# When a modulation chain rests, how the first FFN ends, and who casts the first weight tiles

## The chip, the cores and the metric

The kernel runs on one core of a Trainium2 chip, in one launch. The metric is the device time of a run in microseconds; less is better. The core has TensorE (PE in the profile; PEld is its weight load), VectorE (DVE), ScalarE (ACT), GpSimd (POOL) and SyncE (SP), each of which takes its instructions in order and waits for others by semaphores. SyncE issues nearly all DMAs, from one queue.

## The reference

Two blocks over 256 tokens of width 1024, batch 1, all in float32. The first mixes an mLSTM with a sparse attention and adds a gated projection. The second has two layers; each computes

- `mod = silu(c) @ mod_w[i] + mod_b[i]`, six vectors of 1024, numbered (i, m): 0 and 1 shift and scale the mixer's input, 3 and 4 the FFN's, 2 and 5 gate the two branches
- `hin = x * (1 + mod1) + mod0`, then a mixer: layer 0 MLA (compress `hin` to `c_q` and `c_kv` by one product, rms-normalise them, expand to queries, keys and values, rotary part by a product of its own, causal softmax attention of 8 heads, output product), layer 1 MoBA, which for 256 tokens is causal attention with position penalty
- `x = layer_norm(alpha * x + mod2 * y)`, then `hin = x * (1 + mod4) + mod3`, a convolutional gated FFN of inner width 2816 (`ffn_a`, `ffn_b`, a 3-tap convolution, gelu, product, `ffn_o`), and `x = layer_norm(alpha * x + mod5 * y)`

## The kernel before, in words

Every large product is made of three matmuls: a float32 operand is split into a high half (a cast to fp32r) and a low half (the rest), and high*high + high*low + low*high are accumulated. Weights arrive as tiles of 128x1024 (512 KB), numbered in the order of use by `weight_units` (line 61). For each tile SyncE loads it into a slot of the ring (`load`), ScalarE casts it (`hi`, line 1861), VectorE subtracts (`lo`, line 1330), and TensorE uses it (lines 1099 to 1101). Four to six `parts` hold tiles that are split; a slot of the ring is free again after its `lo`.

The order of all work is one list of steps that `order` (line 102) builds before anything runs; each engine walks the list and issues what is its own, so a step's place in the list is its place in the queue of every engine that it touches. The class `Stream` (`W`) keeps it: `next` is called for the tile wanted now; it first prepares tiles ahead while a part is free (`prepare`: load and `hi`), and emits `lo` until at most `lag` prepared tiles are without one (`low`). `done` gives a part back and calls `step`, which advances the tasks that run beside: each has a rate, and for every whole one that its account reaches, one step of the task is emitted. `W.still` stops the emission while the account goes on.

One such task is `modulation` (the chain): for the vectors (0, 0), (0, 1), (0, 3), (0, 4), (1, 0), (1, 1), (1, 3), (1, 4) it emits eight `mod_v` steps (VectorE, lines 1389 and 1391: the weight tile times a scalar, added to an accumulator), then two empty steps (one in layer 1), `mod_one` with `mod_sum`, and `mod_pe` with `mod_fin`. Its rate is `mod[0][1]`, from `MOD_PACE`. It is 0 from the gate product of the first block on and is set to 0.65 right after `modulated(0, 0)` (line 780). The vectors (i, 2) and (i, 5) are made otherwise: `Between` loads eight `mod_w` tiles and TensorE multiplies them (`mod_k`, line 1182) in the waits around a normalisation, `tiles` saying how many where. One of its loads goes into `R2`, which is free after `mod_one` of (0, 4). `until` forces out what is left of a vector that is needed.

The MLA begins with `modulated(0, 0)` (transposes of x into `XT` with scale and shift), `mla_c` (tiles 76 to 79, row by row, evacuated by `ev_cq`, lines 1794 and 1799), `mla_kr` (tiles 80 and 81, evacuated by `rope`, lines 1806 and 1808), the transposes of `cq` (line 1112) with `xt_s` (ScalarE high, line 1879; VectorE low, line 1349), and `mla_uv` (tiles 82 and 83, evacuated by `ev_v`).

The FFN of layer 0 uses tiles 98 to 163. `LAST` says up to which round the `ffn_o` tiles (`fo` steps) follow a round later; what is left is done in `last`, where the residual `resid` follows each output: `res_m` (line 1754), `res_a` (1763), `res_s` (statistics, 1768), the variance's end (1775, 1778, GpSimd 2207, 1784) and the normalisation `ln_fin` (VectorE 1788, ScalarE 2086). Four outputs (t, cb): row block t of 128 tokens, column half cb. Before, only tiles 162 and 163 were in `last`.

At the start x is rms-normalised (`rms1`: ScalarE 1866 and 1870, VectorE 1336 and 1340, GpSimd 2159), transposed into `XT` (`xt_s`), and tiles 0 and 1 are split by hand: 0 on VectorE alone (1324 and 1330), 1 on GpSimd alone (2147 and 2153). The first product `blk2` takes them in turns: four k of tile 0, four of tile 1, and again. `busy` (line 1120) are matmuls of zeros.

Of the kernel before, what the change touches and what calls it, by code (L numbers as in the profile page):

```python
# [28 lines left out]
LAG = 1  # L29

LAST = [10, 8]
# [70 lines left out]
def order():  # L102
# [34 lines left out]
    class Stream:  # L137
# [25 lines left out]

        def next(self, name, u):
            while len(self.ready) < min(self.at + len(part.uses) - len(lost), len(units)) and part.free:
                self.prepare()
                while len(self.ready) - self.lows > self.lag:
                    self.low()
            while self.lows <= self.at:
                self.low()  # L170
            while self.soon:
                self.soon.pop(0)()
            assert units[self.at][0:2] == (name, u), (units[self.at], name, u)
            self.at += 1
            return self.at - 1, self.ready[self.at - 1][1]
# [80 lines left out]
    def transposed(tag, nk, kind, ks=None, apart=False, filled=()):  # L256
# [15 lines left out]
        for k in ks or range(0, nk, 2):  # L272
            if apart:
                b = banks[k]
                add("tr", tag, k, (1,), b, None)
            else:
                b = bank.get()
                add("tr", tag, k, (0, 1), b, prior("bank", b))
            if kind is None:
                add("xt_hl", tag, k, b)  # L280
                bank.put(b[0])
            elif kind == "s":
                add("xt_s", tag, k, b)
                bank.put(b[0])
            else:
                s = wk.get()
                add("xt_m", tag, k, b, s, prior("wk", s))
                bank.put(b[0])
                pending.append((k, s))
                if len(pending) > 1:  # L290
                    low_part()
        while pending:
            low_part()
# [14 lines left out]
    add("in_b")  # L308
    add("zero")
# [4 lines left out]
    for on in "VG":  # L314
        W.prepare(on)
        W.low(on)
    transposed("u", 8, "s", apart=True, filled=(lambda: add("busy", 1, 5, bz), lambda: add("busy", 2, 5, bz)))
# [353 lines left out]
    def modulated(i, which, v=None, tiles=()):  # L671
# [7 lines left out]
        transposed(f"m{i}{which}", 8, "m", apart=True, filled=(lambda: v.tiles(tiles[1]), lambda: v.tiles(tiles[2])))  # L679
# [33 lines left out]
    def ffn(i):  # L713
# [14 lines left out]
        def last():  # L728
# [15 lines left out]
            for cb in range(2):  # L744
                for j in js[-2:]:
                    piece(0, cb, j)
            for cb in range(2):
                for j in js:
                    piece(1, cb, j)
            for j in js:  # L750
# [29 lines left out]
    mod[0][1] = MOD_PACE[1]  # L780
# [7 lines left out]
    proj_a("m00", 8, "mla_c", 0, 1, ev_cq)  # L788

# [6 lines left out]
    transposed("cq", 4, "s", ks=(2, 0))  # L796

# [57 lines left out]
    modulated(1, 0, late[0], (3, 3, 2))  # L855
# [39 lines left out]
def build(nc, D, out):  # L895
# [4 lines left out]
    with ctx:  # L900
# [400 lines left out]
        def vector(ve):  # L1301
# [15 lines left out]
            for kind, *a in steps:  # L1317
                if kind == "zero":
                    ve.memset(zero, 0.0).then_inc(*done("V", "zero"))
                elif kind == "hi" and a[5] == "V":  # L1320
                    u, slot, p, before, n, _ = a
                    for e in new("V", ("ld", *slot), before):
                        ve.wait_ge(*e)
                    ve.tensor_copy(parts[p[0]][:, 0:n], raw[slot[0]][:, 0:n]).then_inc(*done("V", "hi", u))
# [7 lines left out]
                elif kind == "rms1":  # L1332
# [5 lines left out]
                    for e in new("V", ("rms1_rs", t)):  # L1338
                        ve.wait_ge(*e)
                    ve.tensor_scalar(Y[:, t, 0:512], X[:, t, 0:512], ss[:, t:t + 1], None, MUL).then_inc(  # L1340
                        *done("V", "rms1", t, 0))
# [513 lines left out]
        def scalar(ac):  # L1855
            for kind, *a in steps:
# [5 lines left out]
                elif kind == "rms1":  # L1862
# [5 lines left out]
                    for e in new("A", ("rms1_rs", t)):  # L1868
                        ac.wait_ge(*e)
                    ac.activation(Y[:, t, 512:1024], X[:, t, 512:1024], ACT.Copy, scale=ss[:, t:t + 1]).then_inc(  # L1870
                        *done("A", "rms1", t, 1))
# [546 lines left out]
```

## Time and profile before

| | us |
|---|---|
| median of 3 runs | 918.39 (917.83 to 918.71) |
| profiled execution | 917.69 |
| its span | 915.9 |
| TensorE busy | 880.1 (96%) |
| VectorE busy | 683.6 (75%) |
| ScalarE busy | 450.2 (49%) |
| GpSimd busy | 70.3 (8%) |
| HBM read | 198.71 MB, 218 GB/s over the span |

Busy time of TensorE counts modelled ends of pipelined matmuls, so a matmul's duration in a row (0.39 us at 512 columns) is longer than its distance to the next one. PEclk is the granted clock, 1.00 being 2.4 GHz and 0.50 being 1.2 GHz. The name before L is the engine, L1330 is line 1330. In a timeline the first number is the start in us from the span's start, the second the duration, and in brackets stands how long the engine was idle before and what ended it.

### The profile page before, as it was taken

The numbers are of one execution on the slowest core, as the hardware profiler recorded it, in microseconds if no ns is written. First come the engines' busy times: TensorE is split into PE (matmuls) and PEld (weight loads), VectorE is DVE, ScalarE is ACT, GpSimd is POOL, SyncE is SP. The second block draws the span as 40 slices with busy tenths as digits, with TensorE's granted clock in tenths as the row PEclk, the third lists the DMA queues.
The fourth block names the chain that finished last, engine by engine and source line by source line (L and its number), as shares of the span: only waits on it lengthen the run. The fifth ranks groups of instructions, "written<-read, shape, count | busy, mean of one in ns | idle before, by whom it ended". The sixth has DMA issues, their size and how long they took to land.

```text
span 915.9 us, 14506 instructions
## 1 busy us (share of the span) xinstructions
PE 880.1 (96%) x5776; PEld 760.4 (83%) x5776; DVE 683.6 (75%) x1084; ACT 450.2 (49%) x712; POOL 70.3 (8%) x64
## 2 busy tenths in 40 slices
PE   8999999999999799989999999989999899999996
PEld 7988887667876697779989999868987799999995
DVE  4697788786996887779867767886787876646666
ACT  5563544444545644455544544354554555444550
POOL 2000001000000110011111010010000120100101
PEclk9999999999999999999999999999999999999999
DMA  8855566544957680399957787648724885665601
GB/s 287 325 170 168 201 202 228 167 143 158 325 207 302 233 318 24 120 345 312 378 184 265 265 323 269 219 152 326 234 93 176 335 309 184 204 201 160 208 3 47
DMA packets 56893, 200.74 MB, mean 219 GB/s; under 512 B 6589, under 2 KB 7925, under 8 KB 56825
## 3 DMA queue, kind: packets, MB, share of 16 engines
q1 hardware_dynamic: 55816, 196.63, 61.4%
q0 software_dynamic: 1008, 3.18, 0.9%
q8 instruction: 46, 0.75, 0.3%
q14 instruction: 23, 0.18, 0.1%
HBM read 198.71 MB, written 1.08 MB: 218 GB/s over the span
## 4 chain that ended last, share of the span: by engine, by line
PE 89%; DVE 6%; issue 2%; ACT 1%; DMA 1%; POOL 1%; SPq 0%; DVEq 0%; ACTq 0%
PE ps L1099 27%; PE ps L1100 26%; PE ps L1101 26%; PE ps L1272 3%; PE ps L1293 1%; PE ps L1112 1%; PE ps L1279 1%; DMA ring<-in_w_iq 1%; PE ps L1233 1%; DVE wk L1366 1%; PE ps L1261 1%; DVE X L1763 1%; PE ps L1191 1%; DVE small L1768 0%; PE ps L1253 0%
## 5 line engine op out<-in xcount | busy, mean ns | idle before, releaser
L1099 PE MATMUL ps<-XT,wsp 128*128 128x256 f32 x768 | 217.2, 283 | 4.3 <-DVE XT L1373 3.0
L1100 PE MATMUL ps<-XT,wsp 128*128 128x256 f32 x768 | 214.6, 279 | 0.0
L1101 PE MATMUL ps<-XT,wsp 128*128 128x256 f32 x768 | 214.2, 279 | 0.0
L1330 DVE TENSOR_TENSOR wsp<-ring,wsp 128x1024 fp32r<-128x1024 f32 x130 | 160.5, 1241 | 17.6 <-ACT wsp L1861 17.6
L1861 ACT CAST wsp<-ring 128x1024 fp32r<-128x1024 f32 (+1 forms) x129 | 134.6, 1046 | 64.6 <-PE ps L1101 52.1
L1099 PEld LDWEIGHTS ps<-XT,wsp 128*128 128x128 f32 x768 | 144.0, 188 | 8.5 <-issue 4.2
L1100 PEld LDWEIGHTS ps<-XT,wsp 128*128 128x128 f32 x768 | 144.0, 188 | 0.9
L1101 PEld LDWEIGHTS ps<-XT,wsp 128*128 128x128 f32 x768 | 143.6, 187 | 0.0
L1099 PE MATMUL ps<-wsp,ra 128*128 128x512 f32 x236 | 95.2, 403 | 6.9 <-issue 5.1
L1101 PE MATMUL ps<-wsp,ra 128*128 128x512 f32 x236 | 94.3, 399 | 0.0
L1330 DVE TENSOR_TENSOR wsp<-arena,wsp 128x1024 fp32r<-128x1024 f32 x74 | 92.6, 1256 | 1.7 <-ACT wsp L1861 1.7
L1100 PE MATMUL ps<-wsp,ra 128*128 128x512 f32 x236 | 93.8, 397 | 0.0
L1861 ACT CAST wsp<-arena 128x1024 fp32r<-128x1024 f32 x74 | 77.1, 1045 | 29.8 <-PE ps L1101 29.6
L1311 DVE SCALAR_TENSOR_TENSOR wk<-ps,cols,wk 128x255 f32<-128x255 f32 (+1 forms) x88 | 36.3, 475 | 69.3 <-ACT wk L2125 69.3
L1099 PE MATMUL ps<-XT,ra 128*128 128x256 f32 x288 | 81.4, 283 | 0.0
L1100 PE MATMUL ps<-XT,ra 128*128 128x256 f32 x288 | 80.8, 281 | 0.0
L1101 PE MATMUL ps<-XT,ra 128*128 128x256 f32 x288 | 80.8, 280 | 0.0
L1099 PE MATMUL ps<-wsp,XT 128*128 128x512 f32 x180 | 73.8, 410 | 1.8 <-issue 1.8
L1100 PE MATMUL ps<-wsp,XT 128*128 128x512 f32 x180 | 71.1, 395 | 0.0
L1101 PE MATMUL ps<-wsp,XT 128*128 128x512 f32 x180 | 71.1, 395 | 0.0
L2225 POOL TENSOR_TENSOR ra<-wk,ra 128x512 fp32r<-128x512 f32 x22 | 37.8, 1718 | 297.5 <-ACT ra L2138 297.5
L1099 PEld LDWEIGHTS ps<-wsp,ra 128*128 128x128 f32 x236 | 44.9, 190 | 18.2 <-issue 6.2
(263 smaller groups left out, 1554.4 us busy)
## 6 DMA issues: line engine op xcount, KB each, us to landing
arena<-in_mod_w SPq DMA_DIRECT2D x48, 512.0 KB, 5.7
ring<-in_mod_w SPq DMA_DIRECT2D x44, 512.0 KB, 4.8
ring<-in_ffn_a SPq DMA_DIRECT2D x30, 512.0 KB, 5.1
arena<-in_ffn_b SPq DMA_DIRECT2D x28, 512.0 KB, 4.8
ring<-in_ffn_o SPq DMA_DIRECT2D x27, 512.0 KB, 4.5
arena<-in_ffn_o SPq DMA_DIRECT2D x17, 512.0 KB, 4.9
ring<-in_ffn_b SPq DMA_DIRECT2D x16, 512.0 KB, 5.1
ring<-in_w_moz SPq DMA_DIRECT2D x14, 512.0 KB, 3.6
```

What stands on the lines that cost most here:

```text
L1099: pe.matmul(o, l[0], r[0], start=start, stop=False)
L1100: pe.matmul(o, l[0], r[1], start=False, stop=False)
L1101: return pe.matmul(o, l[1], r[0], start=False, stop=stop)
L1112: ins = pe.transpose(o, src, ID)
L1191: ins = pe.matmul(ps[b[0]][32 * j:32 * j + 32, 0:256], ones[:, 0:32], acc[q][:, j * 256:(j + 1) * 256], start=True, stop=True, tile_positi ...
L1233: ins = pe.matmul(ps[b[0]][:, e_ * n:(e_ + 1) * n], iqT[r, h // 2, t * 128:(t + 1) * 128], ikT[r, 0:n], start=True, stop=True)
L1261: ins = pe.matmul(ps[b[0]][:, 0:257], pb[es[j][0]][:, c:c + 128], mv[:, j, h, 0:257], start=j == 0, stop=j == t)
L1272: ins = pe.matmul(ps[b[0]][:, 0:n], l, r, start=q == 0, stop=q == len(terms) - 1)
L1311: ve.scalar_tensor_tensor(o[:, sh:256], src[:, q * 256:(q + 1) * 256 - sh], scale(tap, q), o[:, sh:256], MUL, ADD).then_inc(*done("V", top ...
L1330: ve.tensor_tensor(w[:, 1024:1024 + n], raw[slot[0]][:, 0:n], w[:, 0:n].bitcast(f32), SUB).then_inc(*done("V", "lo", u, also=[("raw", *slo ...
L1861: ac.copy(parts[p[0]][:, 0:n], raw[slot[0]][:, 0:n]).then_inc(*done("A", "hi", u))
L2225: po.tensor_tensor(gp[g[0]][:, 512:1024], wk[s[0]], gp[g[0]][:, 0:512].bitcast(f32), SUB).then_inc(*done("G", "ffn_lo", i, u, also=[("wk", ...
```

## The change

Five edits.

1. `mod[0][1] = MOD_PACE[1]` moves from ahead of `mla_c` to behind the transposes of `cq`, and `W.lag` is 2 instead of 1 from behind `mla_c` until there.
2. `LAST[0]` is 9 instead of 10: four tiles (160 to 163) are left for `last` of layer 0. There, in layer 0, row block 1 takes its first two tiles tile by tile and gives their parts back, before the other two are taken output by output.
3. `modulated(1, 0)` gets `W.ahead`, which prepares one tile and emits one `low` if a part is free: once after the second group of `mod_k` tiles and once behind the third pair of transposes. Its tiles are divided (1, 4, 3) instead of (3, 3, 2).
4. At the start tile 0 is cast on ScalarE and tile 1 on GpSimd, both behind the rms normalisation; both low halves are VectorE's, the second behind the `xt_s` of the second pair. GpSimd's cast waits for `rms1` of row block 1. Row block 0 of `rms1` is scaled by VectorE alone.
5. Tiles 3 and 4 are loaded at once, behind the constants, and not after the small inputs.

```diff
-LAST = [10, 8]
+LAST = [9, 8]
...
+        def ahead(self):
+            if part.free and len(self.ready) < len(units):
+                self.prepare()
+                self.low()
...
-    def transposed(tag, nk, kind, ks=None, apart=False, filled=()):
+    def transposed(tag, nk, kind, ks=None, apart=False, filled=(), mid=None):
...
                 bank.put(b[0])
+                if mid and k == 2:
+                    mid()
             else:
...
                 if len(pending) > 1:
                     low_part()
+                if mid and k == 4:
+                    mid()
...
     add("in_b")
+    for _ in range(2):
+        W.fetch()
...
-    for on in "VG":
-        W.prepare(on)
-        W.low(on)
-    transposed("u", 8, "s", apart=True, filled=(lambda: add("busy", 1, 5, bz), lambda: add("busy", 2, 5, bz)))
+    W.prepare()
+    first["part", 1] = ("rms1", 1, 0)
+    W.prepare("G")
+    W.low()
+    transposed("u", 8, "s", apart=True, filled=(lambda: add("busy", 1, 5, bz), lambda: add("busy", 2, 5, bz)), mid=W.low)
...
-    def modulated(i, which, v=None, tiles=()):
+    def modulated(i, which, v=None, tiles=(), ahead=lambda: None):
...
-        transposed(f"m{i}{which}", 8, "m", apart=True, filled=(lambda: v.tiles(tiles[1]), lambda: v.tiles(tiles[2])))
+        transposed(f"m{i}{which}", 8, "m", apart=True, filled=(lambda: (v.tiles(tiles[1]), ahead()),
+                                                               lambda: v.tiles(tiles[2])), mid=ahead)
...
+            free = js[:-2] if i == 0 else []
+            for j in free:
+                for cb in range(2):
+                    piece(1, cb, j)
+                W.done(got[j][1])
             for cb in range(2):
-                for j in js:
+                for j in js[len(free):]:
                     piece(1, cb, j)
-            for j in js:
+            for j in js[len(free):]:
                 W.done(got[j][1])
...
     modulated(0, 0, vs.pop(), (3, 3, 2))
-    mod[0][1] = MOD_PACE[1]
...
     proj_a("m00", 8, "mla_c", 0, 1, ev_cq)
+    W.lag = LAG + 1
...
     transposed("cq", 4, "s", ks=(2, 0))
+    mod[0][1], W.lag = MOD_PACE[1], LAG
...
-    modulated(1, 0, late[0], (3, 3, 2))
+    modulated(1, 0, late[0], (1, 4, 3), W.ahead)
```

## Rows read from the trace of the kernel before

**Rows 1.** The page's part 4, the chain that ended last, by engine.
```profile
PE 89%; DVE 6%; issue 2%; ACT 1%; DMA 1%; POOL 1%; SPq 0%; DVEq 0%; ACTq 0%
```
**Rows 2.** Stretches of one microsecond: length, busy time by engine, granted clock, DMA.
```profile
317.00:318.00 1.00, 0.00 (x0) 0.00 (x0) 1.00 (x2) 0.84 (x1) 0.17 (x1) 1.00 0.66 184
318.00:319.00 1.00, 0.00 (x0) 0.00 (x0) 1.00 (x2) 0.00 (x0) 0.00 (x0) 0.56 0.96 393
...
323.00:324.00 1.00, 1.00 (x4) 0.71 (x4) 0.95 (x2) 0.00 (x0) 0.00 (x0) 0.50 1.03 422
```
**Rows 3.** TensorE's timeline, 312 to 331: start, duration, instruction.
```profile
314.51 1.23 PE L1112 MATMUL ps<-cst,arena 128*128 128x128 f32 x8
320.85 0.77 PE L1099 MATMUL ps<-wsp,ra 128*128 128x512 f32 x1 [5.11 <-issue]
...
324.82 0.45 PE L1099 MATMUL ps<-wsp,ra 128*128 128x512 f32 x1
325.12 0.39 PE L1100 MATMUL ps<-wsp,ra 128*128 128x512 f32 x1
...
328.15 0.39 PE L1101 MATMUL ps<-wsp,ra 128*128 128x512 f32 x1
```
**Rows 4.** VectorE's timeline over the same stretch.
```profile
313.82 0.88 DVE L1799 TENSOR_SCALAR arena<-ps,small 128x256 f32<-128x256 f32 x2 [0.82 <-POOL small L2213]
314.62 1.27 DVE L1391 SCALAR_TENSOR_TENSOR R<-ring,cactr,R 128x1024 f32<-128x1024 f32 x1
...
317.28 1.28 DVE L1391 SCALAR_TENSOR_TENSOR R<-arena,cactr,R 128x1024 f32<-128x1024 f32 x1
318.47 1.22 DVE L1330 TENSOR_TENSOR wsp<-ring,wsp 128x1024 fp32r<-128x1024 f32 x1
...
320.27 1.65 DVE L1349 SCALAR_TENSOR_TENSOR ra<-ps,cols,ra 128x256 fp32r<-128x256 f32 x4
```
**Rows 5.** ScalarE's timeline, the high halves of `cq`.
```profile
315.34 1.57 ACT L1879 ACTIVATE ra<-ps,cols 128x256 fp32r<-128x256 f32 x4 [1.69 <-PE ps L1112]
```
**Rows 6.** Two stretches of the MLA's attention.
```profile
345.00:372.00 27.00, 27.00 (x156) 19.88 (x156) 20.94 (x70) 13.58 (x45) 1.41 (x2) 1.00 0.06 21
372.00:382.00 10.00, 9.29 (x50) 7.00 (x49) 6.10 (x15) 5.51 (x15) 0.00 (x0) 1.00 0.02 2
```
**Rows 7.** Timelines of TensorE and of SyncE's queue, 380 to 384.
```profile
383.20 0.40 PE L1099 MATMUL ps<-wsp,ra 128*128 128x512 f32 x1
...
381.30 0.43 SPq L2260 DMA_DIRECT2D arena<-in_ffn_a  x1
```
**Rows 8.** DMA issues near 381.3: count, size, us from issue to landing.
```profile
arena<-in_ffn_a SPq DMA_DIRECT2D x1, 512.0 KB, 4.4
```
**Rows 9.** VectorE's timeline, the residual before the first FFN.
```profile
391.80 0.69 DVE L1754 TENSOR_TENSOR wk<-ps,R 128x512 f32<-128x512 f32 x1 [2.21 <-PE ps L1101]
...
394.59 0.69 DVE L1754 TENSOR_TENSOR wk<-ps,R 128x512 f32<-128x512 f32 x1
```
**Rows 10.** Timelines of TensorE, GpSimd and VectorE at the first FFN's end.
```profile
580.14 0.40 PE L1099 MATMUL ps<-wsp,ra 128*128 128x512 f32 x1
...
582.19 1.56 POOL L2225 TENSOR_TENSOR ra<-wk,ra 128x512 fp32r<-128x512 f32 x1 [15.71 <-ACT ra L2138]
...
583.10 1.73 DVE L1330 TENSOR_TENSOR wsp<-ring,wsp 128x1024 fp32r<-128x1024 f32 x1 [0.51 <-ACT wsp L1861]
...
591.92 0.69 DVE L1754 TENSOR_TENSOR wk<-ps,R 128x512 f32<-128x512 f32 x1
...
598.26 0.55 DVE L1788 TENSOR_SCALAR X<-X,small 128x512 f32<-128x512 f32 x1
```
**Rows 11.** Timelines of VectorE, GpSimd and TensorE at the start.
```profile
10.24 1.23 DVE L1330 TENSOR_TENSOR wsp<-ring,wsp 128x1024 fp32r<-128x1024 f32 x1
10.26 2.10 POOL L2147 CAST wsp<-ring 128x1024 fp32r<-128x1024 f32 x1 [1.18 <-DMA ring<-in_w_iq]
...
14.88 0.39 PE L1099 MATMUL ps<-XT,wsp 128*128 128x256 f32 x1 [1.17 <-POOL wsp L2153]
```

More of the change, by code:

```diff
@@ L1319, in vector @@
                     ve.memset(zero, 0.0).then_inc(*done("V", "zero"))
[L1320 to L1324, printed above, removed]
                 elif kind == "lo" and a[4] == "V":
@@ L1339, in vector @@
                         ve.wait_ge(*e)
-                    ve.tensor_scalar(Y[:, t, 0:512], X[:, t, 0:512], ss[:, t:t + 1], None, MUL).then_inc(
-                        *done("V", "rms1", t, 0))
+                    for c in range(2 - t):
+                        cs = slice(c * 512, (c + 1) * 512)
+                        ve.tensor_scalar(Y[:, t, cs], X[:, t, cs], ss[:, t:t + 1], None, MUL).then_inc(
+                            *done("V", "rms1", t, c))
                 elif kind == "xt_s":
@@ L1867, in scalar @@
                         *done("A", "rms1_sq", t))
[L1868 to L1871, printed above, removed]
+                    if t == 1:
+                        for e in new("A", ("rms1_rs", t)):
+                            ac.wait_ge(*e)
+                        ac.activation(Y[:, t, 512:1024], X[:, t, 512:1024], ACT.Copy, scale=ss[:, t:t + 1]).then_inc(
+                            *done("A", "rms1", t, 1))
                 elif kind == "xt_s":
```

## The prediction

> **What bounds the kernel.** The page comes first: the chain that ended last is 89% TensorE, so a cheaper operation on another engine is worth only the time in which TensorE stands [rows 1]. So the next view is the table of stretches of one and two microseconds, in which I looked for those where TensorE is busy for less than their length. There are few: the first 16 us, the normalisations at 290 to 298, 396 to 404, 592 to 602 and 714 to 721, the end, and one hole of five microseconds at 316 to 321 in which TensorE does nothing and VectorE is never idle [rows 2]. The diff touches three of them: the start, the hole at 316, and the end of the first FFN. In each I laid the timelines of the engines beside the order of the steps and read which wait ends last.
>
> The hole first. TensorE transposes `cq` at 314.51 and its next instruction, the first `mla_uv` matmul, starts at 320.85 [rows 3]. It needs the low half of the transposed `cq` from VectorE (`xt_s`, line 1349), which starts at 320.27 [rows 4]: 0.58 us from that start to the matmul. ScalarE had made the high half for it from 315.34 on [rows 5]. Between, VectorE works off what the step list put in front: a `mod_v` (314.62), a low half, a `mod_v` (317.28), a low half (318.47), the rope.
>
> **Part 1, the modulation chain rests.** The chain's pace stays 0 through `mla_c` and `mla_kr`. Its old pace of 0.65 per finished tile, with the 0.8 that it carries, gave `mod_v` behind tiles 76, 77, 79 and 80: four steps, two of them behind `ev_cq`. Also `W.lag` is 2 over `mla_kr`, so of the two low halves there the second (tile 84) moves behind the transposes. From VectorE's queue between `ev_cq` and `xt_s` go 1.19 (314.62 to 315.81) + 1.19 (317.28 to 318.47) + 1.14 (318.47 to 319.61) = 3.5 us, and ahead of `ev_cq` two more (0.67 + 1.2). What is late next: `ev_cq` ends near 312.8 instead of 314.6, the bias row and the low half of tile 83 take 1.5 and end at 314.3, the rope needs TensorE's end of `mla_kr` (314.5) and is done at 315.4; then both high halves of ScalarE are there at 315.34 + 2 x 0.39 = 316.12. So ScalarE, not VectorE, ends the wait: `xt_s` starts at 316.15 and the matmul at 316.15 + 0.58 = 316.73. TensorE itself is busy until its transposes end, so no more is to be had. Saved: 320.85 - 316.73 = 4.1 us.
>
> The clock adds to this. In the hole the granted clock is 1.00 up to 318 and then 0.50 (1.2 GHz instead of 2.4), and it stays there until 325 with TensorE at work again [rows 2]. The nine matmul steps from 320.85 to 324.82 take 3.97 us; at the full clock 13 steps take 3.03 us, 0.233 each [rows 3], so nine would take 2.10. Two and a half microseconds of idle left the clock at 1.00; the wait that remains is 1.2. I take 1.8 for it (the first step after a wait is a little longer). Together 5.9 us.
>
> What is given back. (a) The four `mod_v` are not gone: by the same count they now fall behind tiles 88, 89, and two attention steps later, in the MLA's attention, 1.19 us each. There VectorE is idle for 6.1 of the 27 us from 345 to 372 and TensorE not at all [rows 6], so an inserted step can be mostly hidden; the small steps of the last vector's end (0.9 us at 367.8) leave this place. TensorE is 5.9 us earlier and VectorE at first only 3 to 3.7, but its short idles up to 338 close most of that. Bounds: nothing, and all four on the path, 4.8. I take 0.5, nearest to the 0.7 us that TensorE waits now from 372 to 382, behind a stretch as dense [rows 6].
> (b) The chain's end, `mod_one` of vector (0, 4), moves from 356.7 to behind tile 93, where TensorE is at 383.20 [rows 7]. SyncE's queue holds the load of `mod_w` tile 40 into `R2` behind it. Before, that load went out right behind `mod_one`; the queue then waited only for the last attention output and sent `ffn_a0` 1 at 381.30, which landed 4.4 us later at 385.7 [rows 7, 8]. Now tile 40 can go at 383.9, it and tile 41 land first, and `ffn_a0` 1 comes at about 383.9 + 3.5 + 2 x 1.25 = 389.9, up to 391.0 by the gaps of the landings before. Its cast (1.05) and its low half (1.14) stand on VectorE ahead of the second half of the residual, which starts at 391.80 [rows 9]; it would start at 392.1 to 393.3. That chain ends its statistics at 394.45 and has 0.1 us to spare before row block 1 begins at 394.59 [rows 9]. The cost is 0.2 to 1.4, I take 0.8. The other FFN tiles are also some 4 us later, but they wait for `XT` until 402.7; tile 104, the tightest, lands at about 409.4 for a cast at 411.3. The end of the chain's small VectorE steps (0.9) fits into 2.2 us of idle before 391.80.
> Part 1: 5.9 - 0.5 - 0.8 = 4.6 us.
>
> **Part 2, the FFN's first layer ends with four tiles.** The tiles come in the same order; only the `fo` matmuls of tiles 160 and 161 move into `last()`, and their second row block behind the first row block's end. The residual's row block 0 then has 2.8 us more of TensorE's work behind it (12 matmuls of 0.233). But tile 162 needs the second gelu product, and GpSimd ends its low half only at 582.19 + 1.56 = 583.75; TensorE, which begins the `fo` matmuls at 580.14, is through tiles 160 and 161 of row block 0 at 582.9 [rows 10]. So it waits 0.95 us, a new stall, and ends its last matmul at 592.25 instead of 591.3. What counts is VectorE's chain: row block 1's residual begins at 591.92, held by VectorE's own queue, and its last normalisation at 598.26 [rows 10]. Now VectorE is through row block 0 at 590, and the residual waits for TensorE's first output of row block 1, 590.85 + 0.2 = 591.05. Gain 0.87. The two `ahead` steps put a low half (tile 165) between the normalisation and the modulation's first scaling, where VectorE idles 0.87 us: 1.14 - 0.87 = 0.27 lost. The second one, and the two casts on ScalarE, fit before tile 167 is wanted; a `mod_v` that is made up for later leaves about 1.3 us at tile 171. The split (1, 4, 3) of the eight modulation tiles moves 0.5 us pieces within waits of TensorE. Net 0.6; bounds -0.5 (the margins go) and 1.8 (no stall).
>
> **Part 3, the start.** `X`'s second half lands at 7.1, so ScalarE's freed 0.7 us buys nothing, and row block 1 is scaled at 9.12 as before. The first tile's cast moves from VectorE (0.69) to ScalarE (1.05), where it starts only at 9.8 and delays the high halves and, on VectorE, its own low half: from 10.24 [rows 11] to 10.88. The second tile's low half leaves GpSimd (12.44 to 14.82) and comes on VectorE behind four `xt_s` (4 x 0.4, by [rows 4]): 10.88 + 1.14 + 1.6 + 1.14 = 14.8. TensorE waited for exactly this tile until 14.88 [rows 11], and would again start near 14.87: nothing. Against it stands the pair VectorE and GpSimd: at 583.10 a low half took 1.73 instead of 1.22 us, and GpSimd's subtraction ended at 583.75, that is VectorE began when GpSimd was done [rows 10]. At the start GpSimd's cast took 2.10 us beginning at 10.26, 0.02 behind VectorE's low half [rows 11]; if it stood until 11.38, alone it takes about 1.0, and the new low half waits for it until 11.26: 0.3 to 0.4 us lost. I take -0.3, bounds +0.3 and -1.4. Two more loads ahead of the small inputs arrive some 4 us earlier; no wait of TensorE there ends with them, so they cost and gain nothing.
> The Trainium skill (SBUF — State Buffer, "SBUF: two separate sides") calls this pair of ports an exclusive lock between a VectorE operation with two SBUF inputs and a GpSimd operation that reads SBUF: who starts first holds it for the whole instruction. The row at 583.10 agrees with it. By the page, which has no duration for this cast, the start would cost between the value taken here and that of the third rival.
>
> **The sum.** 4.6 + 0.6 - 0.3 = 4.9 us off 917.69, the profiled execution's own time (its span of 915.9 and 1.8 around it): 912.8. That execution is 0.7 below the median of the three, so against the median 918.39 the forecast is 913.5.
>
> **Rivals.**
> 1. *The debt comes due.* VectorE is at 80 to 95% in stretches of the attention, and each moved `mod_v` is waited for. For it: the stall at 371 to 376 stands in VectorE's and ScalarE's steps. Against: idle on VectorE in every other stretch. Price 4.8 instead of 0.5: gain 0.6, time 917.8. Chance 0.08.
> 2. *Slower: the load gate.* SyncE's queue stands behind `mod_one`, and what comes later than 383.9 goes one for one into `ffn_a0` 1, its low half and the residual's chain. At 4.9 us later (388.8) the gain is gone. A row product is 2.8 us: behind tile 94 it would be 916.3, behind 95 919.1, and behind 96, or forced out by `until` ahead of the transposes, 8.4 us later, 921.9: this is the rival, slower. For it: the chain starts four steps late and its end has only three more finished tiles before it is forced. Against: the same accounts counted through put its last step one tile behind `mod_one`, two ahead of that. Chance 0.05.
> 3. *The lock at the start*: GpSimd's cast takes its 2.1 us alone too and ends at 12.36, the first tile's low half starts 1.5 us late and TensorE resumes near 16.3: 1.1 more lost, 914.6. Chance 0.15.
> 4. *The hole closes only partly*: something else in VectorE's queue keeps `xt_s` behind 318.3, and the clock drops all the same: gain 2, 916.4. Chance 0.08.
> 5. *Better*: no give-back and no stall in the FFN's end, 910.5 to 911.5. Chance 0.10.
> The forecast itself, 912 to 915, has 0.54.
>
> Range: from the better case to between rivals 4 and 1, 910.8 to 916.8. From no change a measurement here tells 0.2%, 1.8 us; below 916.6 is faster. Faster: the forecast, 3, 4 and 5, 0.87; same: rival 1, 0.08; slower: rival 2, 0.05.
>
> **What would show it.** The wait before the first `mla_uv` matmul about 1.2 us, its clock 1.00, and four `mod_v` fewer before it. SyncE's load into `R2` near 378 (383.9 less the gain) and a later VectorE low half before the second residual half. At the first FFN's end a new wait of about 0.9 us of TensorE for GpSimd's product, and 6.3 us from the residual of row block 1 to the last normalisation. At the start TensorE's second tile within half a microsecond of 14.9. The forecast is wrong if the first is not there, or if TensorE's idle in the attention grows by more than 2 us.

## The result and the profile after

| | us |
|---|---|
| kernel after, median of 4 | 912.74 (911.31 to 913.08) |
| kernel before beside it, median of 4 | 918.55 (917.83 to 920.71) |
| ratio, 95% interval | 0.992 (0.9899 to 0.994) |
| profiled execution after | 911.31, span 909.5 |
| the kernel after again, median of 5 (e9) | 912.42 (911.76 to 912.98), ratio 0.993 (0.9918 to 0.9942) |

Faster by 5.8 us between the medians (the interval of the ratio allows 5.5 to 9.3); the forecast was 4.9 us and 913.5. The chain that ended last, by engine, answers to [rows 1]:

```profile
PE 83%; DVE 11%; issue 2%; ACT 2%; POOL 0%; DMA 0%; DVEq 0%; ACTq 0%
```

VectorE's share grew from 6 to 11%. The growth stands in one place: between 312 and 385 us the chain holds some 44 us of VectorE's pieces, where it held some 5 before. From the hole into the attention the chain that ends last now runs through VectorE, where it ran through TensorE.

**The hole.** Stretches of one microsecond, with the columns of [rows 2]; none has a clock below 1.00:

```profile
317.00:318.00 1.00, 1.00 (x6) 0.81 (x5) 1.00 (x1) 0.00 (x0) 0.40 (x1) 1.00 0.87 356
318.00:319.00 1.00, 1.00 (x6) 0.79 (x5) 1.00 (x2) 0.02 (x1) 0.92 (x2) 1.00 0.25 57
...
323.00:324.00 1.00, 1.00 (x11) 1.00 (x10) 1.00 (x2) 0.31 (x1) 0.00 (x0) 1.00 1.04 406
```

The timelines, which answer to [rows 3 to 5]. VectorE stands idle twice, for TensorE's `mla_kr` and for ScalarE's high half:

```profile
312.29 1.21 DVE L1345 TENSOR_TENSOR wsp<-arena,wsp 128x1024 fp32r<-128x1024 f32 x1
313.73 1.03 PE L1132 MATMUL ps<-cst,arena 128*128 128x128 f32 x8
313.93 0.42 DVE L1823 TENSOR_TENSOR wk<-ps,arena 128x256 f32<-128x256 f32 x1 [0.42 <-PE ps L1121]
...
314.36 1.57 ACT L1897 ACTIVATE ra<-ps,cols 128x256 fp32r<-128x256 f32 x4 [2.15 <-PE ps L1132]
315.31 1.66 DVE L1366 SCALAR_TENSOR_TENSOR ra<-ps,cols,ra 128x256 fp32r<-128x256 f32 x4 [0.63 <-ACT ra L1897]
315.90 0.47 PE L1119 MATMUL ps<-wsp,ra 128*128 128x512 f32 x1 [1.14 <-issue]
```

**The attention**, two stretches against [rows 6], and the two waits in them: TensorE is idle for 0.54 + 1.03 = 1.57 us where it was for 0 + 0.71.

```profile
345.00:366.00 21.00, 20.46 (x109) 14.81 (x109) 17.66 (x55) 11.56 (x41) 0.00 (x0) 1.00 0.00 2
366.00:378.00 12.00, 10.97 (x61) 7.98 (x62) 8.08 (x17) 5.68 (x17) 0.00 (x0) 1.00 0.01 1
...
345.52 0.33 PE L1299 MATMUL ps<-cst,pb 128*128 128x128 f32 x1 [0.48 <-DVE pb L1619]
...
368.40 0.33 PE L1299 MATMUL ps<-cst,pb 128*128 128x128 f32 x1 [0.69 <-DVE pb L1619]
```

Idle time understates this, since busy time counts the modelled ends of matmuls. Laid beside the same matmuls of the kernel before, TensorE's lead falls from 6.80 to 5.93 us over the first wait and by 0.34 more at the second: 1.21 us.

**The load gate**, against [rows 7 to 9]: `mod_one`, SyncE's load into `R`, `ffn_a0` 1, its cast and low half, and the residual's second half, which waits for TensorE, not for them.

```profile
376.80 0.64 PE L1211 MATMUL ps<-R,cst 128*32 128x256 f32 x8
...
377.50 0.33 SPq L2278 DMA_DIRECT2D R<-in_mod_w  x1
...
378.35 0.43 SPq L2278 DMA_DIRECT2D ring<-in_ffn_a  x1
...
383.62 1.05 ACT L1878 CAST wsp<-ring 128x1024 fp32r<-128x1024 f32 x1 [4.79 <-DMA ring<-in_ffn_a]
...
384.71 1.23 DVE L1345 TENSOR_TENSOR wsp<-ring,wsp 128x1024 fp32r<-128x1024 f32 x1 [0.23 <-ACT wsp L1878]
...
386.28 0.69 DVE L1771 TENSOR_TENSOR wk<-ps,R 128x512 f32<-128x512 f32 x1 [0.35 <-PE ps L1121]
```

**The first FFN's end**, against [rows 10]: the new stall, the residual of row block 1, its last normalisation, the second transposes and the first matmul behind them.

```profile
576.66 1.54 POOL L2243 TENSOR_TENSOR ra<-wk,ra 128x512 fp32r<-128x512 f32 x1 [15.71 <-ACT ra L2156]
578.35 0.47 PE L1119 MATMUL ps<-wsp,ra 128*128 128x512 f32 x1 [0.77 <-POOL ra L2243]
...
585.61 0.69 DVE L1771 TENSOR_TENSOR wk<-ps,R 128x512 f32<-128x512 f32 x1 [0.90 <-PE ps L1121]
...
591.79 0.55 DVE L1805 TENSOR_SCALAR X<-X,small 128x512 f32<-128x512 f32 x1
...
592.75 1.06 PE L1132 MATMUL ps<-cst,X 128*128 128x128 f32 x8 [2.32 <-ACT X L2104]
...
595.99 0.47 PE L1119 MATMUL ps<-wsp,XT 128*128 128x512 f32 x1 [0.74 <-issue]
```

**The start**, against [rows 11]: ScalarE's second square, GpSimd's cast, the two low halves, TensorE's first matmul with tile 1.

```profile
6.05 1.06 ACT L1883 ACTIVATE arena<-X 128x1024 f32<-128x1024 f32 x1 [0.31 <-DMA X<-in_x]
...
9.25 1.04 POOL L2165 CAST wsp<-ring 128x1024 fp32r<-128x1024 f32 x1 [1.07 <-DMA ring<-in_w_iq]
...
9.90 1.47 DVE L1345 TENSOR_TENSOR wsp<-ring,wsp 128x1024 fp32r<-128x1024 f32 x1 [1.20 <-ACT wsp L1878]
...
12.86 1.21 DVE L1345 TENSOR_TENSOR wsp<-ring,wsp 128x1024 fp32r<-128x1024 f32 x1
...
14.13 0.38 PE L1119 MATMUL ps<-XT,wsp 128*128 128x256 f32 x1 [0.51 <-DVE wsp L1345]
```

### The profile page after: what moved, and what is told of

It is laid out like the page before. It is cut to its first block, busy times and chain, and to the rows that moved or that the text cites. A ratio compares the mean times of both kernels' runs of the same rounds, so it can differ in the third digit from the quotient of the medians.

```text
span 909.5 us, 14508 instructions
## 1 busy us (share of the span) xinstructions
PE 878.8 (97%) x5776; PEld 759.1 (83%) x5776; DVE 684.0 (75%) x1085; ACT 449.4 (49%) x712; POOL 68.7 (8%) x63
## 4 chain that ended last, share of the span: by engine, by line
PE 83%; DVE 11%; issue 2%; ACT 2%; POOL 0%; DMA 0%; DVEq 0%; ACTq 0%
PE ps L1119 26%; PE ps L1120 25%; PE ps L1121 25%; PE ps L1292 2%; DVE wsp L1345 1%; PE ps L1313 1%; DVE R L1408 1%; DVE small L1610 1%; PE ps L1132 1%; PE ps L1253 1%; DVE wk L1383 1%; PE ps L1281 1%; PE ps L1211 1%; DVE pb L1601 0%; PE ps L1273 0%
## 5 line engine op out<-in xcount | busy, mean ns | idle before, releaser
L1345 DVE TENSOR_TENSOR wsp<-ring,wsp 128x1024 fp32r<-128x1024 f32 x144 | 179.1, 1251 | 9.4 <-ACT wsp L1878 9.3
L1878 ACT CAST wsp<-ring 128x1024 fp32r<-128x1024 f32 x143 | 148.7, 1045 | 59.3 <-PE ps L1121 52.3
L1345 DVE TENSOR_TENSOR wsp<-arena,wsp 128x1024 fp32r<-128x1024 f32 x61 | 75.2, 1238 | 7.5 <-ACT wsp L1878 7.5
L1878 ACT CAST wsp<-arena 128x1024 fp32r<-128x1024 f32 x61 | 63.7, 1046 | 29.6 <-PE ps L1121 26.7
L2029 ACT ACTIVATE pb<-pb,small 128x128 f32<-128x128 f32 (+1 forms) x48 | 21.9, 456 | 74.3 <-DVE small L1610 74.3
```

The costliest lines, as they stand in the source:

```text
L1345: ve.tensor_tensor(w[:, 1024:1024 + n], raw[slot[0]][:, 0:n], w[:, 0:n].bitcast(f32), SUB).then_inc(*done("V", "lo", u, also=[("raw", *slo ...
L1878: ac.copy(parts[p[0]][:, 0:n], raw[slot[0]][:, 0:n]).then_inc(*done("A", "hi", u))
L2029: ac.activation(p, p, ACT.Exp, bias=nmx[:, i:i + 1], accum_out=smx[:, i:i + 1]).then_inc(*done("A", "exp", task, i))
```

## How the parts are told apart

One part is worth a microsecond or less, and single executions differ by more. So besides the medians, each profile is cut at TensorE's groups of transposes, which every kernel has, and the lengths between them are compared (from the timelines; `cq`: the transposes of `cq`; `m01` and `m10`: the second group of those names; `m11`: the first group). From `m11` to the end all take 201.4 to 201.5 us. The last column leaves out the stretch at 0.50 at the end of each profile (3.4 us before its end in the kernel after, 5.4 in e12), in which TensorE has no work left.

| kernel | to `cq` | `cq` to `m01` | to `m10` | to `m11` | stretches at clock 0.50 |
|---|---|---|---|---|---|
| before | 314.51 | 85.12 | 199.59 | 115.14 | 318 to 325 |
| after | 313.73 | 80.38 | 198.64 | 115.31 | none |
| e1 rest alone | 316.16 | 80.49 | 199.58 | 115.88 | 597 to 601 |
| e2 FFN end alone | 314.11 | 84.66 | 198.59 | 115.31 | 320 to 324 |
| e3 start alone | 314.06 | 85.07 | 199.50 | 116.56 | 317 to 325, 693 to 697 |
| e4 pace alone | 314.09 | 80.00 | 199.23 | 115.14 | none |
| e5 debt at once | 315.11 | 83.52 | 201.40 | 116.63 | 338 to 342, 584 to 588, 601 to 605 |
| e7 no ahead | 314.97 | 80.77 | 198.54 | 118.72 | 690 to 694 |
| e8 no last | 313.88 | 80.44 | 201.10 | 116.72 | 399 to 403, 591 to 595, 690 to 694 |
| e9 after again | 314.90 | 80.03 | 198.63 | 116.16 | 593 to 597 |
| e10 lag one | 313.83 | 80.51 | 198.63 | 116.09 | 594 to 598 |
| e11 fill | 313.88 | 80.64 | 197.86 | 116.74 | 686 to 690 |
| e12 fill and hum | 314.74 | 79.99 | 198.34 | 116.51 | 687 to 691 |

Kernels whose chain runs on take 84.66 to 85.12 in the second column, those where it rests 79.99 to 80.77 (without e5, which pays the debt at once): the means differ by 4.6 us. The FFN's new end is in the third column: 198.54 to 198.64 against 199.23 to 199.59, 0.87 us between the means (left out are e5 and e8, for the clock, and e11 and e12, for their own edits there). By the columns 4.6 + 0.9 us of the gain are placed, of which 0.2 goes again behind `m10`; the half microsecond that is left to 5.8 has no place in them and is inside the scatter of the medians. e6, which changes the second column by itself, is told below.

## Experiments

The kernels were timed in four groups, each on one chip and with the kernel before beside it: e1 to e4, e5 to e8, e9 to e11, and e12. The kernel before had medians of 918.21, 918.51, 918.33 and 918.72 there.

**e1, the chain's rest alone.** The kernel before with

```diff
-    mod[0][1] = MOD_PACE[1]
...
     proj_a("m00", 8, "mla_c", 0, 1, ev_cq)
+    W.lag = LAG + 1
...
     transposed("cq", 4, "s", ks=(2, 0))
+    mod[0][1], W.lag = MOD_PACE[1], LAG
```

> The kernel before with the first edit alone: the modulation chain rests until cq is split, and W.lag is 2 over mla_kr. My theory: all of the large gain is here. The wait before the first mla_uv matmul falls from 6.3 us to about 1.1, the granted clock stays 1.00 through it, and the run is 4.2 to 5.4 us below the kernel before (5.9 won, some 1.2 given back in the attention). The start and the end of the first FFN look as in the kernel before: a transpose of m10 some 5.5 us earlier and none of it from the FFN. Rival: the clock term is not real or is given back whole, and only the length of the hole counts: 3 to 4 us. Second rival: the three edits lean on each other (the FFN's end only pays with the chain's debt elsewhere), then this one alone gives more than 5.5 or less than 3.

Measured: 913.63 us (912.75 to 917.0), ratio 0.995 (0.993 to 0.9969), 4.6 us off. The profiled execution took 915.45, and the excess is its start: `cq` comes 2 us later than in e2 and e4, which have the same start. There tile 1 landed early, and GpSimd and VectorE met:

```profile
9.15 1.34 DVE L1341 TENSOR_SCALAR arena<-X,small 128x512 f32<-128x512 f32 x1 [0.67 <-POOL small L2160]
9.17 1.04 POOL L2148 CAST wsp<-ring 128x1024 fp32r<-128x1024 f32 x1
10.29 2.41 POOL L2154 TENSOR_TENSOR wsp<-ring,wsp 128x1024 fp32r<-128x1024 f32 x1
10.41 2.84 DVE L1325 CAST wsp<-ring 128x1024 fp32r<-128x1024 f32 x1
```

VectorE's cast takes 0.69 us elsewhere; begun 0.12 us behind GpSimd's subtraction it ends 0.55 us behind that one's end.

**e2, the FFN's end alone.** The kernel before with `LAST = [9, 8]`, the tile-by-tile beginning of row block 1, `W.ahead` and the tiles (1, 4, 3).

> The kernel before with the second edit alone: LAST[0] is 9, row block 1 begins tile by tile, W.ahead twice and modulation tiles 1, 4, 3. My theory: 0.6 to 1.0 us faster. A new wait of TensorE of 0.8 to 0.95 us for GpSimd's half of the gelu product (line 2153 or its subtraction for the FFN) near 581 to 583, VectorE's last normalisation of row block 1 about 6.2 us behind the residual of row block 1, which waits for TensorE. Rival: the gain seen after the whole change comes from the chain of small VectorE steps standing elsewhere, and alone this edit gives nothing (within 0.3 us) or loses the 0.8 of its stall.

Measured: 917.34 us (915.89 to 921.67), ratio 0.9993 (0.9978 to 1.0008). The 0.9 us between the medians is inside the interval; the third column shows it (198.59).

**e3, the start alone.** The kernel before with the casts, the low halves, the early loads and the undivided row block 0 of `rms1`.

> The kernel before with the third edit alone: first tiles cast on ScalarE and GpSimd, both low halves on VectorE, tiles 3 and 4 loaded early, row block 0 of rms1 on VectorE alone. My prediction had 0.3 us slower; the trace after the change has the start 0.77 us faster. Theory A (the landing): the second half of X landed 1.05 us earlier in that execution by luck; where it lands at 7.1 as in the kernel before, the start is even (between 0.4 slower and 0.1 faster), TensorE's second tile at 14.7 to 15.2 and the time within 0.5 us of the kernel before. Theory B (the Copy): ScalarE's second square could not begin before its Copy of row block 0 ended (7.06), and the removed Copy is what lets it begin at the landing: then TensorE's second tile begins near 14.1 and the run is 0.6 to 0.9 us faster, with the second square starting at 6.0 to 6.1. Both want GpSimd's cast at about 1.04 us, as it does not stand beside a VectorE subtraction.

Measured: 918.07 us (917.27 to 919.1), ratio 0.9996 (0.9986 to 1.0006). Theory B was right about the square (6.04 us) and wrong about the time: tile 1 begins at 14.43, as late as with the old start in e2 (14.42) and e4 (14.45). The three parts alone give 4.6 + 0.9 + 0.1 = 5.6 us against 5.9 together (e9): they add up, as far as intervals of one to two microseconds can tell.

**e4, the pace alone.**

```diff
-    mod[0][1] = MOD_PACE[1]
...
     transposed("cq", 4, "s", ks=(2, 0))
+    mod[0][1] = MOD_PACE[1]
```

> As the first of these, but W.lag stays 1: the low half of tile 84 stays in VectorE's queue ahead of the rope. My theory: VectorE has 0.42 and 0.63 us of idle there after the change, so of the 1.14 us of that low half only 0.1 to 0.3 us is late: the hole's wait is 1.2 to 1.5 us and the run as the first of these within 0.3 us (the lag edit is worth almost nothing). Rival: the low half goes one for one into the wait (1.14 us): wait 2.2 us, run 1.1 us above the first of these; at that length of idle the clock still holds by my theory, for TensorE stood 2.5 us in the kernel before at granted clock 1.00.

Measured: 912.67 us (911.76 to 912.88), ratio 0.9931 (0.9916 to 0.9946). Two low halves now stand ahead of the rope, and TensorE's wait is 1.14 us as after the change:

```profile
312.68 2.35 DVE L1330 TENSOR_TENSOR wsp<-arena,wsp 128x1024 fp32r<-128x1024 f32 x2
314.09 1.03 PE L1112 MATMUL ps<-cst,arena 128*128 128x128 f32 x8
...
316.26 0.47 PE L1099 MATMUL ps<-wsp,ra 128*128 128x512 f32 x1 [1.14 <-issue]
```

So the lag edit buys nothing in this wait. The nine matmul steps behind the hole take 2.19 us here (316.26 to 318.45) against 3.97 in the kernel before: 1.78 us for the clock.

**e5, the debt at once.** The kernel after with

```diff
     mod[0][1], W.lag = MOD_PACE[1], LAG
+    mod[0][2] += 2.6
```

> The kernel after the change, with 2.6 added to the chain's account where it starts again: the four mod_v that fell due while it rested come all at once behind tile 82, and mod_one of (0, 4) two tiles earlier (behind 91). My theory: the debt costs where it stands close to work that TensorE waits for. In the kernel after it costs about 0.9 us between 345 and 378 (TensorE's idle there beyond that of before). Four in a row (3 x 1.2 + 0.7 = 4.3 us of VectorE) stand ahead of a low half and of ev_v, while TensorE has two to three tiles of mla_uv (2.8 us each) in hand: 1 to 3 us of TensorE's idle between 318 and 330, little less idle later: 913.5 to 915.5. Rival (debt is free anywhere): VectorE's idle takes it, and the attention's 0.9 us comes back: 911.5 to 912.7.

Measured: 919.37 us (915.59 to 921.35), ratio 0.9994 (0.9977 to 1.0011): the whole gain is gone, more than I had forecast. The wait isn't at 318 to 330 but ten microseconds on. TensorE's waits from 312 to 396 (us in total, times, longest), and GpSimd's sum for the queries' rotary part, late behind VectorE:

```profile
PE ps L1293 <- POOL arena L2238: 2.5, 1, 2.5
```

```profile
334.41 1.22 DVE L1346 TENSOR_TENSOR wsp<-ring,wsp 128x1024 fp32r<-128x1024 f32 x1
...
335.55 0.42 DVE L1824 TENSOR_TENSOR wk<-ps,arena 128x256 f32<-128x256 f32 x1
...
336.45 2.40 POOL L2238 TENSOR_TENSOR arena<-wk 128x256 f32<-128x256 f32 x2 [16.06 <-DVE wk L1826]
...
337.22 0.48 PE L1293 MATMUL ps<-arena 64*128 64x128 f32 x2 [2.54 <-POOL arena L2238]
```

Behind it the clock stands at 0.50 from 338 to 342, and `m01` is 3.1 us later by the second column. The third column has 2.8 more: at the FFN's end GpSimd's low half took 2.72 us, with two steps of VectorE beside it, so that the stall was 1.95 us, and the clock fell again. There a `mod_v` (from 580.40) and the low half behind it (581.59 to 582.81) both went ahead of GpSimd's, which began at 581.21. In the kernel after no `mod_v` stands there; that the debt's early payment put one there was not tried.

**e6, the late gate.** The kernel after with `MOD_PACE = [0.8, 0.55, ...]`.

> The kernel after the change with the chain's pace 0.55 instead of 0.65 behind cq: mod_one of (0, 4) stands behind tiles 96 and 97, the last of mla_o, instead of behind 93. This is the mechanism of my rival 2 by itself. It says: SyncE's load into R2 (377.5 after the change) goes some 8 us later, ffn_a0 1 lands 8 us later than 383.6, and its cast and low half, which stand ahead of the second half of the residual, hold the normalisation: some 8 us slower than the kernel after, 920 to 921.5, with TensorE's second group of transposes of m01 at 401 to 403 instead of 394.1. Counter-theory: SyncE's late load is made up for, since the first tiles of the FFN are only needed behind the normalisation and the ring has room: under 2 us slower, 912.5 to 914.7.

Measured: 929.72 us (928.9 to 931.58), ratio 1.0117 (1.0096 to 1.0139), 17.3 us above e9, twice the price I had put on it. The longest wait of TensorE from 312 to 410, and the steps that lead to it:

```profile
PE ps L1220 <- ACT msum L1927: 16.5, 1, 16.5
```

```profile
388.63 0.33 SPq L2278 DMA_DIRECT2D R<-in_mod_w  x1
...
394.91 1.04 ACT L1878 CAST wsp<-arena 128x1024 fp32r<-128x1024 f32 x1 [16.96 <-DMA arena<-in_ffn_a]
...
397.13 0.68 DVE L1771 TENSOR_TENSOR wk<-ps,R 128x512 f32<-128x512 f32 x1
...
404.66 0.35 ACT L1927 COPY msum<-ps 128x256 f32<-128x256 f32 x1
405.06 0.69 PE L1220 MATMUL ps<-cst,msum 128*128 128x128 f32 x2 [16.49 <-ACT msum L1927]
```

The load goes 11.1 us later than after the change (388.63 against 377.50), the residual's second half follows 10.9 later (397.13 against 386.28): the rival's mechanism, which had put 8 us on it. The rest, 6.4 us, it had not seen: the chain's own end (`msum` on ScalarE) stands behind cast and normalisation in the queue, TensorE's row products wait for it, and they run at clock 0.50 (391 to 408).

**e7, without ahead.** The kernel after with `modulated(1, 0, late[0], (3, 3, 2))`: two parts of the edit are undone at once, `W.ahead` and the split (1, 4, 3).

> The kernel after the change without W.ahead and with modulation tiles 3, 3, 2 as before; the four tiles at the FFN's end stay. My prediction put 0.27 us of loss on the low half between the normalisation and the first scaling and nothing on the rest. By that this is 0 to 0.3 us faster (912.4 to 912.8), TensorE's first matmul after m10 about 0.3 earlier. Rival: ahead is what pays, since it fills VectorE's queue ahead of tile 166 and 167: without it a wait of 0.5 to 1.3 us for VectorE appears between 596 and 610 and the run is 0.5 to 1.2 us slower.

Measured: 915.76 us (913.31 to 916.79), ratio 0.996 (0.9946 to 0.9974), 2.8 us above e9 by the ratios: the rival, and larger. Of it 1.9 us are a wait for a low half, which `ahead` brings forward (that the split has no part in it wasn't tried apart); a stretch at 0.50 stands behind 690 as well:

```profile
601.00 2.35 DVE L1345 TENSOR_TENSOR wsp<-ring,wsp 128x1024 fp32r<-128x1024 f32 x2
...
602.28 0.50 PE L1119 MATMUL ps<-wsp,XT 128*128 128x512 f32 x1 [1.92 <-DVE wsp L1345]
```

**e8, without the four tiles.** The kernel after with `LAST = [10, 8]`.

> The kernel after the change with LAST[0] back at 10: two tiles at the FFN's end, ahead and the split 1, 4, 3 stay. My prediction put +0.87 on the four tiles (residual row block 1 earlier), after a new stall of 0.95 of TensorE. By that this is 0.9 us slower than the kernel after (913.6 to 914.0), the wait for GpSimd at 577.6 is gone, the last normalisation of row block 1 comes 0.9 us later than at 591.8, and TensorE's wait before the second transposes of m10 grows by about 0.5. Since TensorE then idles near 2.9 us there, I also expect the granted clock to fall behind that wait in some executions, as it did once with the chain's rest alone (0.50 from 597 to 601). Rival: the new stall eats the gain and the time does not change (within 0.3 us).

Measured: 914.17 us (913.35 to 915.4), ratio 0.9946 (0.9927 to 0.9965), 1.5 us above e9 by the ratios, whose intervals overlap. GpSimd's stall is gone, and in its place TensorE waits 1.81 and 0.82 us at `m10`; the clock fell there and in two more places. How much of the 1.5 is the four tiles and how much the clock, this run doesn't tell.

**e9, the kernel after again.**

> The kernel after the change itself, timed beside the next two on one chip, for their comparison and for what one execution's start and clock are worth. By the profiles so far it has no stretch at granted clock 0.50 of its own, so executions differ by the start (the landing of tile 1 and of X, 1.0 us between them) and by short stretches at 0.50 that come and go: 911.5 to 913.5, some 5.5 us below the kernel before. If the first four executions were lucky, it is above 914.

Measured: 912.42 us. A stretch at 0.50 that the first profile lacked stands behind the wait before `m10`; the second group of transposes takes 1.88 us instead of 1.06:

```profile
593.56 1.88 PE L1132 MATMUL ps<-cst,X 128*128 128x128 f32 x8 [2.32 <-ACT X L2104]
```

**e10, the lag at one.** The kernel after without `W.lag = LAG + 1`.

> The kernel after the change with W.lag left at 1 over mla_kr. Theory from the chain's rest with and without the lag edit (from the transposes of cq to those of m01 77.2 us with it, 76.8 without): the low half of tile 84 is hidden ahead of the rope and its absence behind cq lets VectorE come up sooner: 0.3 to 0.5 us faster than the kernel after, wait before mla_uv unchanged at 1.14 us. Rival: the 0.4 is chance, no difference.

Measured: 911.67 us (911.0 to 912.3), ratio 0.9924 (0.9912 to 0.9935). `cq` to `m01` is 80.51, within the 79.99 to 80.77 of the kernels that rest, with either lag (79.99 to 80.51 with lag 1, 80.03 to 80.77 with lag 2). Neither the 0.4 us nor the difference of the medians can be told from chance.

**e11, a piece in the stall.** The kernel after with

```diff
+            free = js[:-2] if i == 0 else []
+            if free:
+                piece(1, 0, free[0])
             for cb in range(2):
                 for j in js[-2:]:
                     piece(0, cb, j)
-            free = js[:-2] if i == 0 else []
             for j in free:
-                for cb in range(2):
+                for cb in range(j == free[0], 2):
                     piece(1, cb, j)
```

> The kernel after the change, with one of row block 1's pieces (the first column half of tile 160, three matmuls, 0.7 us) moved ahead of tile 162 of row block 0 at the first FFN's end, where TensorE waits 0.77 us for GpSimd's half of the gelu product. My theory: the wait falls to about 0.1, row block 0's residual stays where it is, and row block 1's starts at its queue's end, 0.7 us earlier (VectorE idle 0.90 before it now): the last normalisation, the second transposes of m10 and the time 0.6 to 0.8 us earlier. Rival: VectorE's chain is bound elsewhere (its idle moves behind the normalisation) and the time stays within 0.2 us.

Measured: 912.24 us (911.05 to 912.61), ratio 0.9928 (0.9916 to 0.9939). The wait for GpSimd is gone from the list of waits, VectorE's idle before row block 1's residual is 0.19 instead of 0.90 us, and `m01` to `m10` takes 197.86 instead of 198.64: 0.78, as expected. In the medians it is 0.2, inside the scatter.

```profile
585.24 0.69 DVE L1773 TENSOR_TENSOR wk<-ps,R 128x512 f32<-128x512 f32 x1 [0.19 <-PE ps L1123]
```

**e12, both, and matmuls in the wait.** e10 and e11 together, and in the wait before `m10` twelve of the `busy` matmuls:

```diff
+    def hum():
+        b = bank.get()
+        add("busy", 3, 12, b, prior("bank", b))
+        bank.put(b[0])
...
-filled=(lambda: (v.tiles(tiles[1]), ahead()),
+filled=(lambda: (v.tiles(tiles[1]), ahead(), (i, which) == (1, 0) and hum()),
```

> The kernel after the change with three edits: W.lag stays 1 over mla_kr, one piece of row block 1 (the first column half of tile 160) goes ahead of tile 162, and twelve matmuls whose result nobody reads stand in the wait of 2.32 us before the second transposes of m10. Theory: by the profiles the piece is worth 0.77 us, the lag nothing. The matmuls are there for the clock: in six of nine profiled executions with the chain at rest, or with the FFN's new end, a stretch of 3.5 to 4.5 us at 0.50 begins within 4 us of that wait (584 to 597 us) or behind the next group of waits (686 to 690), each worth some 1.5 us; with TensorE at work in the wait the first of the two should be gone from the profile and the executions' mean clock at 0.997 or 0.998: median 910.8 to 911.6, against 912.4 of the kernel after. Rival (the clock's short stretches do not hang on this wait): the profile has one all the same near 593, mean clocks 0.995 to 0.997, median 911.7 to 912.2. Second rival (the added matmuls are in the way): the second transposes of m10 start later than 0.77 us before those of the kernel after, by up to 0.5 us.

Measured: 911.09 us (910.16 to 912.84), ratio 0.9912 (0.9894 to 0.9931), the lowest of all kernels, though its interval overlaps that of e9.

```profile
590.29 2.94 PE L1146 MATMUL ps<-arena 128*128 128x128 f32 x24
593.07 1.04 PE L1138 MATMUL ps<-cst,X 128*128 128x128 f32 x8
```

The wait is filled, the profile has no stretch at 0.50 near 593, and three of six executions have a mean clock of 0.998 or 0.999 (e9: none of five above 0.997). That is no proof: the first profile of the kernel after had no such stretch either, and the mean clock also counts the stretch at the end, which costs nothing. The other stretch, at 687 to 691, stays. The matmuls are also in the way: `m01` to `m10` is 198.34, 0.48 more than in e11, as the second rival said. The twelve (two records each) took 2.94 us in a wait of 2.32; whether fewer would do wasn't tried.

## Why the prediction was right, step by step

- **The hole, 4.1 us.** From the transposes of `cq` to the first `mla_uv` matmul 2.17 us were measured, 2.22 forecast, 6.34 before: right, and for the named reason, ScalarE's high halves. That the second low half had to leave the queue was part of my account and was wrong (e4, e10): VectorE had 0.42 + 0.63 = 1.05 us of idle there. The four `mod_v` are the whole cause: e4 removes them alone and has the same 2.17 us.
- **The clock, 1.8 us.** Right (1.78 by e4), and none of the eleven profiles with the chain at rest has a clock below 1.00 at the hole. But the ground for it, that 2.5 us of idle had left the clock at 1.00, is weaker than it looked: behind waits of 2.32 us and less it fell in some executions (last section). Over all profiles the chain's rest is worth 4.6 us between `cq` and `m01`, which is the term of the sum.
- **What is given back, 0.5 + 0.8.** The sum, 1.3, came out at 1.2 by luck: two wrong parts cancelled. The attention costs 1.21, not 0.5, and the load gate nothing, not 0.8: `ffn_a0` 1 lands 6.1 us behind the load into `R`, as forecast (6.0), but the residual's second half waits for TensorE 0.35 us longer than for that tile's low half. Hole and clock, 4.17 + 1.78, less 1.21 are 4.74, which is what this pair of profiles has in the second column (85.12 - 80.38). The step that was mis-sized is (a): VectorE's idle of 6.1 us was taken to hide the debt, but VectorE had just become the engine behind which TensorE waits (11% of the chain).
- **The FFN's end, 0.6 us.** The stall was 0.77 for 0.95 (0.25 of it GpSimd's own wait for VectorE, last section), and `m01` to `m10` is 0.87 shorter; the first matmul then comes 3.24 us behind the second transposes where it came 3.05 behind them. Net 0.7. The step that failed here is the one on `ahead`: I charged it 0.27 and gave it nothing, and without it and its split the new end loses 1.9 us to a late low half (e7). With it the low half of tile 165 cost no more than the pair of measurements can tell (198.64 with, 198.54 without).
- **The start, -0.3 us.** Measured nothing that can be told (e3: between 1.3 faster and 0.6 slower). "`X`'s second half lands at 7.1, so ScalarE's freed 0.7 us buys nothing" was wrong. 7.11 comes right behind the end of ScalarE's Copy (6.34 + 0.72) in the kernel before. With the Copy gone the square begins when the data lands (6.05 us, idle before it and released by the DMA), and in the ten profiles with the new start that was 5.84 to 6.05 six times and 6.59 to 7.28 four times. What that wins, the second low half on VectorE spends. Tile 1 begins at 14.13 to 15.22 (mean of ten 14.63) against 14.42 to 14.88 of three old starts and some 2 us later in the fourth (e1). So the sign "within half a microsecond of 14.9" failed in the kernel after (14.13) and in two more of the ten.
- **The rivals.** 3 (the lock at the start) was refuted by every profile: GpSimd's cast takes 1.04 us where VectorE does not hold it up. 1 and 2 did not happen as priced (a quarter of 1 did, 1.2 us of 4.8), but e5 and e6 show that both stand close: the same four `mod_v` at once cost the whole gain, and a pace of 0.55 instead of 0.65 costs 17 us. I had priced them at 4.3 and 8.4; the missing part was each time what a long wait sets off: the clock, and steps queued behind.

## What to carry to other kernels

A background task that shares VectorE should rest while TensorE waits for the end of a short chain there, and its debt should be paid back one step at a time: the same four steps cost 1.2 us spread out and about 6 us more in one place. Before a wait is priced, look whether the row before it ends just there: at a start without an idle time in brackets the engine came straight from its own work, and when the data landed can't be read from it. And where a wait of TensorE goes or comes, look at the clock behind it and price that too, and count the steps that stand behind the late one in each queue.

## What the hardware showed

- **Short stretches at clock 0.50.** With TensorE's work and waits the same, some executions have a stretch of 3.5 to 4 us at 0.50 and others don't: behind the wait of 2.32 us at `m10` in e9 and e10, not in the first profile of the same kernel; behind waits of 0.5 and 1.2 us near 684 and 686 in e11, not after the change. From `m10` to `m11` a profile without one takes 115.14 us with the old end of the FFN and 115.31 with the new one; one with a stretch takes 0.7 to 1.4 us more. The two profiles of the kernel after differ by 1.7 us in all: 1.17 by the start and 0.85 by such a stretch, less 0.35 between `cq` and `m01`. What decides whether the clock falls stays open.
- **GpSimd beside VectorE.** GpSimd's cast of 128x1024 took 1.04 us, and its subtraction of 128x512 took 1.29 (at 398.70 after the change) when VectorE had nothing under way. Begun while VectorE subtracted or cast from SBUF, it took its own time plus what was left of VectorE's instruction, less 0.15: the cast 2.10 with 1.21 us left [rows 11], 1.89 with 1.00 left (e10), 1.47 with 0.58 left (e4), 1.16 with 0.28 left (e2); the subtraction at the first FFN's end 1.54 with 0.40 left, as in the kernel before. VectorE pays alike: 1.73 for 1.22 with 0.65 left of GpSimd's [rows 10], 2.84 for 0.69 with 2.29 left (e1). So the second one waits for the first instead of sharing. The rule of the Trainium skill (SBUF — State Buffer, "SBUF: two separate sides"), that the one that starts first holds the shared ports for its whole instruction, agrees with all of these but for the 0.15. Recorded starts that lie 0.02 us apart don't tell who is first: in e1 VectorE's scaling is recorded at 9.15 and GpSimd's cast at 9.17, and VectorE was the one held (1.34 us for 0.49).
